# Two post-norm layers of a hybrid decoder on one core: softmax division moved in its slot, convolution taps dealt anew, the first norm's residual scaled on ScalarE and its total summed from SBUF

## What is computed

```python
# attention of mixers A and B, per head and per 128 queries
s = q . k * scale, masked;  pr = softmax(s);  y = pr @ v
# mixer C
h = a * sigmoid(g);  h = depthwise_conv(h, conv_w, width 31, causal) + conv_b;  y_c = silu(layer_norm(h))
gates = sigmoid(gate_pre + b_gate)
merged = gates[0]*(y_a @ w_branch[0]) + gates[1]*(y_b @ w_branch[1]) + gates[2]*(y_c @ w_branch[2])
x = layer_norm(ALPHA * x + merged @ w_out, ln1_g, ln1_b)          # the first norm
ffn = (silu(f_gate) * f_up) @ w_ffn_out;  ple = sigmoid(x @ w_ple_gate) * (p_i @ w_ple_proj)
x = layer_norm(ALPHA * x + ffn + ple, ln2_g, ln2_b)               # the second norm
```

## Time and profile before

| | us |
|---|---|
| median of 3 runs | 1850.85 |
| lowest and highest | 1849.95, 1851.07 |
| the profiled execution | 1852.88 |
| its span, first to last instruction | 1851.1 |
| TensorE busy | 1811.0 |
| VectorE busy | 1065.1 |
| ScalarE busy | 813.2 |
| GpSimd busy | 771.2 |

### The profile page before, as it was taken

How to read it: one execution, slowest core, us unless ns; L and a number is a source line. 1 busy time by engine, 2 the same in 40 slices (tenths; PEclk the granted TensorE clock), 3 DMA queues, 4 the chain that set the end, 5 groups by cost and what they waited for, 6 DMA issues and landing times.

```text
span 1851.1 us, 25182 instructions
## 1 busy us (share of the span) xinstructions
PE 1811.0 (98%) x8654; PEld 1502.9 (81%) x8654; DVE 1065.1 (58%) x1965; ACT 813.2 (44%) x1431; POOL 771.2 (42%) x336
## 2 busy tenths in 40 slices
PE   9999999999999999999999999999999999999997
PEld 9887787878778888888897877888887888888885
DVE  6379999868973111203254999997889711111033
ACT  4544777743433232322244457777434322322222
POOL 5443223345354444444444522233543544444541
PEclk9999999999999999999999999999999999999998
DMA  5322111223233332333333321122232332333331
GB/s 185 103 95 88 46 58 58 70 69 103 82 112 102 91 101 92 101 103 103 101 95 91 108 75 46 58 64 63 83 103 79 112 100 93 94 99 101 103 103 57
DMA packets 47032, 166.04 MB, mean 90 GB/s; under 512 B 5472, under 2 KB 5728, under 8 KB 46944
## 3 DMA queue, kind: packets, MB, share of 16 engines
q1 hardware_dynamic: 46080, 163.60, 28.3%
q10 hardware_dynamic: 864, 1.28, 0.2%
HBM read 162.76 MB, written 2.10 MB: 89 GB/s over the span
## 4 chain that ended last, share of the span: by engine, by line
PE 69%; issue 12%; DVE 9%; POOL 5%; ACT 4%; DMA 0%; DVEq 0%; POOLq 0%; ACTq 0%; SPq 0%
PE banks L829 18%; PE banks L831 18%; PE banks L830 18%; POOL sb_wl L453 4%; PE banks L880 3%; PE banks L882 3%; PE banks L881 3%; PE banks L936 2%; PE banks L986 2%; DVE sb_work L1267 1%; DVE sb_top L1265 1%; ACT sb_pbuf L564 1%; ACT sb_pbuf L571 1%; ACT sb_wh L526 1%; DVE banks L1319 1%
## 5 line engine op out<-in xcount | busy, mean ns | idle before, releaser
L453 POOL TENSOR_TENSOR sb_wl<-sb_wraw,sb_wh 128x1024 fp32r<-128x1024 f32 x303 | 743.8, 2458 | 1039.1 <-ACT sb_wh L526 1038.8
L829 PE MATMUL banks<-sb_xh,sb_wh 128*128 128x512 f32 x1344 | 540.6, 402 | 2.8 <-POOL sb_wl L453 1.8
L831 PE MATMUL banks<-sb_xh,sb_wl 128*128 128x512 f32 x1344 | 525.1, 391 | 0.0
L830 PE MATMUL banks<-sb_xl,sb_wh 128*128 128x512 f32 x1344 | 524.3, 390 | 0.0
L526 ACT ACTIVATE sb_wh<-sb_wraw 128x1024 fp32r<-128x1024 f32 x303 | 319.6, 1055 | 281.3 <-PE banks L831 175.1
L831 PEld LDWEIGHTS banks<-sb_xh,sb_wl 128*128 128x128 f32 x1344 | 252.2, 188 | 54.5
L829 PEld LDWEIGHTS banks<-sb_xh,sb_wh 128*128 128x128 f32 x1344 | 253.2, 188 | 52.9 <-issue 5.1
L830 PEld LDWEIGHTS banks<-sb_xl,sb_wh 128*128 128x128 f32 x1344 | 253.2, 188 | 41.3
L1319 DVE SCALAR_TENSOR_TENSOR banks<-sb_hconv,sb_par,banks 128x512 f32<-128x512 f32 x232 | 172.2, 742 | 1.5
L829 PE MATMUL banks<-sb_hh,sb_wh 128*128 128x512 f32 x352 | 137.7, 391 | 0.0
L831 PE MATMUL banks<-sb_hh,sb_wl 128*128 128x512 f32 x352 | 137.0, 389 | 0.0
(11 more groups left out here) (294 smaller groups left out, 2936.3 us busy)
## 6 DMA issues: line engine op xcount, KB each, us to landing
sb_wraw<-in_weights SPq DMA_DIRECT2D x304, 512.0 KB, 3.6
sb_u<-in_x SPq DMA_DIRECT2D x8, 256.0 KB, 6.3
out<-sb_u SPq DMA_DIRECT2D x8, 256.0 KB, 2.0
sb_praw<-in_ple ACTq DMA_DIRECT2D x2, 512.0 KB, 4.3
sb_par<-in_params ACTq DMA_DIRECT2D x2, 98.5 KB, 2.5
sb_rope_tmp<-in_freq ACTq DMA_DIRECT2D x1, 24.0 KB, 4.4
sb_small<-in_pos ACTq DMA_DIRECT2D x1, 2.0 KB, 4.1
```

Source lines behind the costliest of these rows:

```text
L453: nc.gpsimd.tensor_tensor(wl[:, t % WS, :], wraw[:, t % 2, :], wh[:, t % WS, :].bitcast(F32), ALU.subtract).then_inc(lo_ready, 1)
L829: nc.tensor.matmul(out, wh_, xh_, start=start, stop=False)
L830: nc.tensor.matmul(out, wh_, xl_, start=False, stop=False)
L831: return nc.tensor.matmul(out, wl_, xh_, start=False, stop=stop)
```

## The change

In attention, ScalarE's division of unit n moves from the middle of slot n+1, where it stood behind the exponential of unit n+1, to the head of slot n+1, ahead of the copies and gates of that slot. VectorE's reciprocal of unit n moves likewise from behind the mask of unit n+1 to ahead of it. The taps are dealt otherwise: 47 instead of 55 in slots 0 to 31, and 77 instead of 69 in slots 32 to 63; slots 0 to 12 keep one each.

In the first norm, ScalarE scales `xh` by ALPHA into `u` (eight instructions, in two groups of four ahead of the rounding of tiles `T_OUT`+3 and `T_OUT`+4), and VectorE only adds ALPHA*`xl`, behind a wait for the new semaphore `scaled`. In both norms, each block but the last is now added to `total` from `u` in SBUF after its `arrive`, instead of the residuals of blocks 4 to 7 at once after `arrive(4)` and the PSUM banks of blocks 5 to 7 singly. Block 7 is still added in two parts, `u` ahead and the bank at the end. That is 16 + 4 instructions fewer on VectorE in the first norms of both layers, 4 fewer in the second norms, and 16 more on ScalarE.

```diff
--- before.py
+++ after.py
@@ -123,7 +123,10 @@
 KEEP_SLOT = len(SELECT_LATE) // 2
 TAPS_AT, _taps = [], 0
 for _slot in range(UNITS):
-    _n = 1 if _slot <= KEEP_SLOT else 3 if (_slot - KEEP_SLOT) % 5 == 4 else 2
+    if _slot < UNITS // 2:
+        _n = 1 if _slot <= KEEP_SLOT or _slot % 5 == 4 else 2
+    else:
+        _n = 3 if _slot % 5 in (0, 2) else 2
     TAPS_AT.append(range(_taps, min(_taps + _n, CK * CW)))
     _taps = TAPS_AT[-1].stop
 assert _taps == CK * CW
@@ -206,7 +209,7 @@
         CONV_PLACE[(T_CONV if _j < 2 else T_U + 2) + 2 * _j + _v] = (_j, _v)
 
 
-V_FRONT, V_ATTN, V_CONV, V_LN1, V_LN2, V_PG, V_FI = 127 - len(SELECT_LATE), 129 + len(SELECT_LATE), 5, 40, 24, 8, 2
+V_FRONT, V_ATTN, V_CONV, V_LN1, V_LN2, V_PG, V_FI = 127 - len(SELECT_LATE), 129 + len(SELECT_LATE), 5, 30, 22, 8, 2
 VS_ATTN = V_FRONT
 VS_CONV = VS_ATTN + V_ATTN
 VS_LN1 = VS_CONV + V_CONV
@@ -377,6 +380,7 @@
         u_ready, shift_sum, shift_ready, shifted, squared, sum_ready, sq_summed = (
             sem("u_ready"), sem("shift_sum"), sem("shift_ready"), sem("shifted"), sem("squared"), sem("sum_ready"),
             sem("sq_summed"))
+        scaled = sem("scaled")
         mean_ready, sq_ready, var_ready, warmed, sd_ready, diag_ready, spread, mean_spread = (
             sem("mean_ready"), sem("sq_ready"), sem("var_ready"), sem("warmed"), sem("sd_ready"), sem("diag_ready"),
             sem("spread"), sem("mean_spread"))
@@ -601,19 +605,17 @@
                         turned_probabilities(n)
                         if n + TURN_LAG < UNITS:
                             exponentials(n + TURN_LAG)
-                        if n + 1 < UNITS:
-                            probabilities(n + 1)
                     elif kind == "score" and n < TURN_LAG:
                         exponentials(n)
-                        if n == 1:
-                            probabilities(0)
                     elif kind == "value":
                         value_part(n)
-                    elif kind == "slot" and n == KA_SLOT:
+                    elif kind == "slot" and 1 <= n <= UNITS:
+                        probabilities(n - 1)
+                    if kind == "slot" and n == KA_SLOT:
                         nc.scalar.activation(ka_h[:], ka_t[:], ACT.Copy).then_inc(ka_high, 1)
                         nc.scalar.activation(idx_r[:, :, G_VA - AD:G_VA], h_idx[:, :, G_VA:G_VA + AD],
                                              ACT.Copy).then_inc(va_high, 1)
-                    elif kind == "slot" and n in Y_SPLIT:
+                    if kind == "slot" and n in Y_SPLIT:
                         c = Y_SPLIT[n]
                         if c == 0:
                             act.wait_ge(turn_out, turns + (TURN_AT[("prep", ("A", 3), "")] + 1))
@@ -769,6 +771,8 @@
                 act.wait_ge(tile_used, first + (T_OUT + START))
                 nc.scalar.activation(ph[:], praw[:], ACT.Copy).then_inc(p_high, 1)
                 for k in range(DK):
+                    for j in {0: range(4), 1: range(4, DK)}.get(k, ()):
+                        nc.scalar.activation(u[:, j], xh[:, j].bitcast(F32), ACT.Copy, scale=ALPHA).then_inc(scaled, 1)
                     high(T_OUT + k + LEAD, first)
                     for j in range(3) if k == 4 else (3, 4) if k == 5 else range(k - 1, k) if k > 5 else ():
                         squares(layer, 0, j)
@@ -1354,10 +1358,10 @@
                 steps.wait()
                 last_conv_input()
                 for slot in range(UNITS + NORM_LAG):
+                    if 1 <= slot <= UNITS:
+                        inverse(slot - 1)
                     if slot < UNITS:
                         mask(slot)
-                    if 1 <= slot <= UNITS:
-                        inverse(slot - 1)
                     if slot >= NORM_LAG and (slot - NORM_LAG) % 2:
                         combine((slot - NORM_LAG) // 2)
                     taps = list(TAPS_AT[slot]) if slot < UNITS else []
@@ -1433,23 +1437,16 @@
                 for j in (2, 3):
                     steps.done(v.tensor_tensor(total, total, u[:, j], ALU.add))
                     steps.wait()
-                arrive(4)
-                dve.wait_ge(u_ready, x0 + (5 + 2))
                 for j in range(4, DK):
-                    steps.done(v.tensor_tensor(total, total, u[:, j], ALU.add))
-                    steps.wait()
-                for k in (1, 2, 3):
-                    add_square(k)
-                for j in range(IN_BANK, DK):
+                    arrive(j)
                     if j < DK - 1:
-                        dve.wait_ge(tile_used, first + (tile(j) + 1 + START))
-                        steps.done(v.tensor_tensor(total, total, psum[:, 2 + j % 2, :], ALU.add))
-                        steps.wait()
-                        arrive(j)
+                        dve.wait_ge(u_ready, x0 + (j + 1 + 2))
+                        for i in (j,) if j < DK - 2 else (j, DK - 1):
+                            steps.done(v.tensor_tensor(total, total, u[:, i], ALU.add))
+                            steps.wait()
                     else:
-                        arrive(j)
                         v.tensor_tensor(total, total, psum[:, 2 + j % 2, :], ALU.add).then_inc(sum_ready, 1)
-                    for k in {5: (4,), 6: (5, 6), 7: (7,)}[j]:
+                    for k in {4: (1, 2, 3), 5: (4,), 6: (5, 6), 7: (7,)}[j]:
                         add_square(k)
 
                 mean, scale, by_mean, by_square = [psum[:, b, :] for b in (STAT[n], STAT[n] + 1, STAT[n] + 1, 2)]
@@ -1654,8 +1651,7 @@
                 def residual(j):
 
                     if j < DK:
-                        steps.done(v.tensor_scalar(u[:, j], xh[:, j].bitcast(F32), ALPHA, None, ALU.mult))
-                        steps.wait()
+                        dve.wait_ge(scaled, layer * DK + (j + 1))
                         steps.done(v.scalar_tensor_tensor(u[:, j], xl[:, j].bitcast(F32), ALPHA, u[:, j], ALU.mult,
                                                           ALU.add))
```

## The result

| | before | after |
|---|---|---|
| median, us | 1850.93 (6 runs) | 1857.41 (6 runs) |
| lowest to highest | 1849.82 to 1851.15 | 1857.04 to 1857.98 |
| span of the profiled execution | 1851.1 | 1855.2 |

The ratio is 1.0036, with an interval of 1.0025 to 1.0047: the change makes the kernel about 6.5 us slower. The prediction of 1842.2 (1836.5 to 1848.0) was wrong, also in its sign. Beside the lines shown with the change, these come up in the rows after: the low part of the turned probabilities L1301, transposes L940, value products L990, the copies of the queries L556 and L557 (VectorE's part of them is L1341).

What follows compares the result with a forecast made beforehand. TensorE, busy 1811.0 of 1851.1 us, was taken as the bound, except for VectorE early in attention. 2 x (2.6 attention + 1.7 first norm) = 8.6 us off 1850.85 gave 1842.2, range 1836.5 to 1848.0.

Steps and rivals of the forecast that it cites:

- The bound of each part: Attention of layer 0: VectorE bounds 167 to 212 us, TensorE 212 to 272 and 272 to 366 us.
- The division's own wait: Attention, 272 to 366 us: TensorE's waits for the division and the restarts behind them vanish, 1.8 + 1.0 = 2.8 us.
- upper bound of 3.1: Attention: gain of 2.6 us a layer, with bounds of 0.3 and 3.1.
- signs of being right: Attention, 272 to 366 us: no L936 wait for the division, TensorE idle under 1 us, VectorE busy over 92 us.
- Rival 4: Attention slot heads: VectorE and ScalarE wait for each other, exponential included; 4.0 us longer a layer, 1855.4 us; chance 0.08.
- new waits of TensorE for L1297: Attention: sign of being wrong, new waits of TensorE for L1297 or L1305 after slot 45.
- The taps: Attention: eight fewer in slots 0 to 31, seven more in slots 32 to 62; 0.5 us of new waits.
- level: Attention, 272 to 366 us: VectorE's 92.6 us of work against 92.9 available; late by 1 to 2 us towards the end.
- The first norm: `arrive(4)` wait 1.3 us instead of 2.65, last total's wait 1.2 us, token sums 1.7 us sooner a layer.
- rival 1: First norm: no collisions, residual 7 not held, wait and clock fall go; 4.4 us a layer, 1836.8 us; chance 0.15.
- the clock: First norm, at `arrive(4)`: whether it still falls left open; a fall costs 1.75 us, gain then 1.2 instead of 1.7.
- The sum: Both layers: attention 2.6 and first norm 1.7 us, twice, 8.6 us faster, 1842.2 us; chance 0.50.

Runs made afterwards that it cites:

- e10: The change with the division behind the copy of the turned probabilities on ScalarE (copy, division, exponential) and the taps dealt as before: 1841.8 us, ratio 0.9950.
- e9: The change with one edit, the division behind the copy of the turned probabilities on ScalarE (copy, division, exponential): 1842.5 us, ratio 0.9963.
- e4: The whole change with the taps dealt as in the kernel before: ratio 1.0023, 4.2 us slower than before, 1855.0 us.
- e1: The kernel before with only the first norm's and the totals' part of the change, attention as before: 1850.3 us, ratio 0.9999.
- e8: e1 with three filler products more ahead of the token sums in the first norm: 1848.1 us, ratio 0.9986.
- e13: e10 with three filler products more ahead of the token sums in the first norm: 1841.9 us.
- e14: e13 with three more filler products between the mean's token sums and the squares': 1841.6 us.
- e3: The kernel before with only the taps dealt anew, order and norm as before: 1852.6 us, ratio 1.0011.

## Why the prediction was wrong

**The bound of each part**: right. TensorE is idle for 0.00 us in the second part after the change (60.00 busy of 60), `combine` is still a wait of the first.

**The division's own wait, 2.8 us a layer**: right in size, at another place. The waits for it sank from 1.8 to 0.7 us in the third part of after, and in e10, where nothing takes their place, units 32 to 63 took 90.3 us instead of 93.0. From unit 0 to the branches e10 gains 4.0 us a layer, more than the upper bound of 3.1: the first half of attention gives 0.8 of it, the last slots behind unit 63 0.6.

**The step that failed** is one sentence: "ScalarE waits for the reciprocal at the same place, with a copy, a gate and a tile's rounding behind; gates and tiles have slots to spare." It names three instructions behind the wait and gives a reason for two. The copy was left out, and it has no slot to spare: the low part needs it in the same slot, and every second slot the value products behind that. The step also took ScalarE's idle time (74.19 us busy of 94) as free to move; but its 20.0 us of waits for transposes over the whole of attention were what kept the copy on time. In their place came 46.9 us of waits for the reciprocal with the copy behind them, new waits of TensorE for L1301 (5.2 us from 272 to 366 us), and attention 5.1 us a layer longer instead of 2.6 shorter. The signs of being right named there failed with it: TensorE idle for 6.45 us and not under 1, VectorE busy for 90.4 us of 99.1 and not over 92.

**Rival 4, a loop at the head of the slot** (0.08): right in kind and close in time, 1855.4 for 1857.4, but with the wrong instruction in it. It closed the loop over the exponential, found margins of 0.75 us there, and was marked down for them. Those margins held: no wait of VectorE's reciprocal for L568 is among after's waits. The loop closes over the copy, which the margins say nothing of. Its cost of attention was 4.0 us a layer; 5.1 were measured. The sign listed for it that did appear is "new waits of TensorE for L1297", the first at 289.80 us and so well before slot 45.

**The taps**: the reasoning held, the size did not. New waits of 0.5 us were taken for the third part; with the order of e9 and e10, which has no loop, the new taps cost 1.9 us, and with the loop more (1.6 us of interplay). Eight taps fewer ahead of slot 32 gave nothing with that order, 105.7 us in e9 and 105.8 in e10, but 1.6 with the order of the change, 105.8 in after and 107.4 in e4. A VectorE busy for 89.4 of 92.2 us is no longer "level" with TensorE, since it can't use each gap.

**The first norm**: nearly all as walked. `arrive(4)`: 1.23 us of wait for a forecast of 1.3. The last total: 0.84 for 1.2. Token sums 27.0 us after tile 3 for 27.4, a gain of 2.1 a layer for 1.7. Residual 7 was held (the pair L1655 took 3.50 us for 1.4) by GpSimd's subtraction from 472.99 to 475.5, and so was square 4, 2.78 us. Earlier in the same stretch two residual adds took 3.48 us beside GpSimd's subtraction from 468.19 to 470.9. That speaks against rival 1. The trace agrees with the rule of the Trainium skill, page SBUF — State Buffer, section SBUF: two separate sides, that the shared port pair is locked for a whole instruction and that a VectorE operation with two SBUF inputs takes part. **What failed here** is the clock: the question was put at `arrive(4)`, where it no longer fell, and not at the next place where TensorE has little to do. There it fell in both layers of e1, e4, e8, e10 and e13 and cost 1.7 us a layer (from the first output product to the feed-forward's output 349.8 us in e10, 348.1 in e9), 3.3 in layer 0 of e1, so the 4 us of the norm became 0.4 in e1. In after it did not fall in either layer, and the norm's gain is whole in its 1857.4. By the marks, the change without it would be some 4 us worse; no run has the new order and the new taps with the old norm.

**The sum**, with what was measured: attention −5.1, norm +2.05, twice −3.05, 6.1 us slower by the marks; 6.5 by the medians. The two profiled executions differ by only 4.2 us (1852.88 and 1857.04). The one of before lies 2 us above its median, and the stretch from the first product of layer 1's feed-forward output to the end took it 140.5 us, for 139.0 in after: its clock was at half for 3.4 us behind the token sums of the last norm, and that of after was not.

## What to carry to other kernels

When a step is moved ahead in an engine's queue, list every instruction that comes to stand behind its wait and ask of each who needs its result in the same round; the one that feeds the engine you wait for closes a loop, and its price grows with how full that engine is. An engine's idle time for the tensor engine's results is often what keeps it punctual, not slack that a wait elsewhere can use up. Where a move pays off with an engine relieved (8.8 us faster) and costs with it full (5.0 slower), look first for a place one instruction later: here it turned the 6.5 us lost into 8 gained, by the medians.

## What the runs showed of the hardware

In the first norm TensorE makes 16 one-column products, 1.8 to 2.3 us long. With the new norm its clock fell to half behind them in both layers of e1, e4, e8, e10 and e13 and in layer 1 of e14, although nothing but 0.17 us of idle time stood ahead of them in e8 and e13. It did not fall there in after, in e9, or in layer 0 of e14. With the old norm, which has no idle time ahead of the same products, it fell there in none of the nine kernels, but in one layer or both of each behind the wait for `arrive(4)`, as in before. In layer 0 of e3 it fell at neither place, with the same wait of 2.65 us. Behind the token sums of the second norm it fell only in layer 1 of before and of e3. So which kernel it hits changed with edits elsewhere. A gain of 2 us at one place can be given back at the next stretch of small products, and one profile with a fall or without isn't the property of an edit.
